# Hybrid encoder layer on one core: the expert row table built in fewer, larger steps and the last norm divided among three engines

## Chip, cores and metric

One core of a Trainium2 chip runs the whole program. The metric is the device time of one execution in microseconds, as the median of several runs.

## The reference, cut to what matters

The program is one layer of a streaming encoder over 1088 tokens (1024 of a prompt, 64 of a running stream) of width 1024, all in float32. Two token mixers (a state-space model and a sparse attention) end in a first layer norm. Behind it stands the part that the change touches:

```python
scores = sigmoid(x @ w_router)                       # 64 experts
idx    = top_k(scores + router_bias, 6)
gate   = scores[idx] / sum(scores[idx]) * 2.5
# each expert's rows are padded to whole blocks of 128 rows; one block uses one expert
out    = swiglu(x_pad[row_tok], w_exp_gu[e], w_exp_down[e]) * row_gate
routed = zeros.at[row_tok].add(out)
shared = swiglu(x, w_sh_gu, w_sh_down)
y      = layer_norm(ALPHA * x + routed + shared, ln2_g, ln2_b)
```

## The kernel before, in words

The five engines (PE, VectorE as DVE, ScalarE as ACT, GpSimd as POOL, and SyncE, whose queue SP issues most DMAs) each run an instruction list written by hand, and meet through semaphores. Tokens lie in NT = 9 tiles of 128 rows (the last has 64). The time from the first layer norm on has three stages.

**Shared tiles and row table.** For each tile i, PE multiplies the tile by the shared expert's first weights (`shared_up`, line 818), ACT takes the SiLU of one half, DVE multiplies by the other half (`gate_shared`, line 2122), PE turns the product (`turn_hidden`, line 800), ACT copies it out, PE multiplies by the second weights (`shared_down`, line 809), and DVE adds the result to x (`add_shared`, line 2139), after which SP stores the tile into `acc_d` in DRAM. PE's list is skewed: its pass i holds `shared_up(i+1)`, `turn_hidden(i-1)` and `shared_down(i-1)`.

Between these steps the table of rows is made. DVE first computes a slot for each (token, expert) pair (`slots`, `block_and_place`, lines 2178 to 2187). The slots become one-hot matrices: 54 products (6 picks of 9 tiles), for each of which DVE writes two parts (lines 2225 and 2226) and POOL one (line 1243) into a ring of 12 buffers, and PE adds them up in PSUM (line 856). From the thirteenth product on, DVE and POOL wait until PE has used the buffer that they overwrite. `planned_in(i)` says which products belong to DVE's pass i: 11 in each pass from pass 2 on, so that the last ten fall into pass 6, and into PE's pass 7. Then DVE copies the finished table out (line 2200), PE spreads it over partitions (line 866), DVE makes the row indices (lines 2207 and 2191), and POOL gathers the rows of the first blocks from DRAM by indirect DMA, four DMAs for one block (line 1259). DVE turns gathered rows with 32x32 transposes (`turn_rows`, line 2236).

**Expert loop.** Some 68 blocks, each with 16 matmuls of the first weights (`gate_and_up`, line 883), two transposes (line 889) and 8 matmuls of the second weights (line 897). SP loads 3 MB of weights for each block: the first weights of the block after next when PE is done with the buffer (`egu_full`), the second ones behind the previous block's last matmul. POOL gathers the rows of the coming block and adds the finished one to `acc_d` by an indirect DMA (line 1253).

**Last norm.** SP loads the nine tiles of `acc_d` back (`acc_loaded`). DVE makes mean and variance (`bn_stats` line 2065, `bn_aggr` line 2067, adding EPS line 2068), ACT the square root, DVE the reciprocal and shift (lines 2072 and 2073), ACT scales and shifts the tile (line 1610), DVE multiplies by `ln2_g` (line 2280), POOL adds `ln2_b` (line 1301), and SP stores the tile. All ACT instructions are put down to the helper's line 1307, and SP's loads to line 919.

The buffers `xg` and `xgT` (gathered rows and turned rows) lie over `x1T`, which the shared tiles read, so the first `turn_rows` stands behind the last `add_shared`. The one-hot ring is at offset 27712 of the arena:

```python
xg = [at(0, 4, 2 * P), at(1024, 4, 2 * P)]
xgT = [at(2048, DK, P), at(3072, DK, P)]
onehot = at(27712, 12, P + 2 * NBP)
```

## Time and profile before

| | |
|---|---|
| Median of 3 runs | 2145.34 us (2141.27 to 2145.65) |
| Profiled execution | 2142.77 us |
| Its span on the profile | 2140.8 us |
| PE busy | 1997.9 us (93%) |
| DVE, ACT, POOL busy | 972.6, 562.8, 617.2 us |
| DMA | 365.09 MB, mean 171 GB/s |
| Mean granted PE clock | 0.973 |

The span is one execution; its rows are in microseconds from the start of the span. A row of a timeline gives the start, the length, the engine, the line and the tiles, and in brackets how long the engine was idle before it and which instruction released it. Where several equal instructions are merged, "x8" is their number. PE's matmuls in float32 appear as two records for each product.

### The profile page before, as it was taken

How to read it: one execution, taken by the hardware profiler on the slowest of the kernel's cores; microseconds unless marked ns; L12 is line 12 of the kernel's file. 1: busy time of each engine (PE TensorE's matmuls, PEld its weight loads, DVE VectorE, ACT ScalarE, POOL GpSimd, SP SyncE). 2: the span in 40 equal slices, each digit the busy share in tenths (PEclk: the TensorE clock that was granted, in tenths of full speed). 3: DMA queues.
4: the chain of work that ended last, by engine and by line, in shares of the span. 5: the costliest groups of instructions: out<-in, count | busy, mean ns of one | idle time of the engine just before them, and what ended most of it. 6: DMA issues, size and time to landing. Idle time of an engine off the chain costs nothing.

```text
span 2140.8 us, 23579 instructions
## 1 busy us (share of the span) xinstructions
PE 1997.9 (93%) x7670; PEld 1105.0 (52%) x7670; DVE 972.6 (45%) x2561; ACT 562.8 (26%) x1136; POOL 617.2 (29%) x792
## 2 busy tenths in 40 slices
PE   8999999999999999998999798999999999999980
PEld 6786645666656665565454363444444444444430
DVE  4373465999755551240355543333323332333326
ACT  2224553661666630130223000111111111111112
POOL 0051000011210001101223253455555455545534
PEclk9999999999999999999999899999999999999995
DMA  5040212110100012024211403999999999999994
GB/s 184 3 46 5 62 40 99 40 50 0 32 19 2 1 45 55 19 94 126 111 67 53 155 30 113 362 374 372 374 380 376 374 372 375 378 374 373 372 336 176
DMA packets 130467, 365.09 MB, mean 171 GB/s; under 512 B 34641, under 2 KB 82514, under 8 KB 112594
## 3 DMA queue, kind: packets, MB, share of 16 engines
q1 hardware_dynamic: 105250, 289.80, 36.0%
q0 software_dynamic: 23328, 72.90, 13.1%
q10 hardware_dynamic: 1808, 1.33, 0.2%
q8 instruction: 48, 0.79, 0.2%
q14 instruction: 33, 0.27, 0.0%
HBM read 310.82 MB, written 53.04 MB: 170 GB/s over the span
## 4 chain that ended last, share of the span: by engine, by line
PE 54%; DMA 19%; DVE 9%; issue 7%; POOL 6%; ACT 3%; POOLq 0%; SPq 0%; DVEq 0%; ACTq 0%
DMA arena<-x_d,tid 17%; PE psum L606 11%; PE psum L747 8%; PE psum L765 6%; PE psum L621 4%; POOL arena L1259 3%; ACT arena L1307 3%; PE psum L428 3%; PE psum L818 2%; POOL acc_d L1253 2%; DVE arena L2236 2%; PE psum L682 2%; PE psum L701 2%; PE psum L463 2%; PE psum L474 2%
## 5 line engine op out<-in xcount | busy, mean ns | idle before, releaser
L1307 ACT ACTIVATE arena<-psum 128x512 f32<-128x512 f32 (+8 forms) x641 | 285.1, 485 | 1162.5 <-PE psum L883 436.0
L883 PE MATMUL psum<-arena 128*128 128x512 f32 x1088 | 486.1, 600 | 32.4 <-DVE arena L2236 25.9
L883 PEld LDWEIGHTS psum<-arena 128*128 128x128 f32 x1088 | 201.8, 190 | 273.9 <-issue 273.9
L1259 POOL DMA_INDIRECT arena<-x_d,tid x276 | 265.6, 962 | 83.2 <-issue 71.1
L897 PE MATMUL psum<-arena 128*128 128x512 f32 x544 | 244.7, 592 | 0.5 <-ACT arena L1307 0.5
L606 PE MATMUL psum<-arena 128*128 128x384 f32 (+1 forms) x768 | 239.7, 471 | 0.1
L2242 DVE TENSOR_TENSOR arena<-arena,psum 128x256 f32<-128x256 f32 x68 | 28.6, 421 | 462.6 <-ACT arena L1307 462.6
L606 PEld LDWEIGHTS psum<-arena 128*128 128x128 f32 x768 | 144.2, 190 | 95.4 <-issue 11.4
L747 PE MATMUL psum<-arena 128*128 128x384 f32 (+1 forms) x576 | 178.9, 474 | 5.9 <-DMA arena<-in_w_attn_proj 5.9
L2236 DVE STREAM_TRANSPOSE arena<-arena 128x256 f32<-128x256 f32 x272 | 150.2, 610 | 55.2 <-DMA arena<-x_d,tid 54.2
L897 PEld LDWEIGHTS psum<-arena 128*128 128x128 f32 x544 | 103.3, 190 | 130.3 <-issue 129.6
L1855 DVE TENSOR_SCALAR_CACHE_REDUCE arena<-arena 128x512 uint8<-128x512 f32 (+6 forms) x175 | 154.8, 929 | 2.0
L747 PEld LDWEIGHTS psum<-arena 128*128 128x128 f32 x576 | 110.7, 193 | 73.3 <-DMA arena<-in_w_attn_proj 6.4
L1265 POOL TENSOR_TENSOR carry<-ones 1x1 f32<-1x1 f32 x135 | 53.6, 397 | 314.1 <-DMA acc_d<-arena,sid 279.3
L1307 ACT ACTIVATE arena<-arena 128x896 uint8<-128x896 f32 (+1 forms) x99 | 110.5, 1117 | 77.6 <-DVE arena L1901 48.8
L1217 POOL TENSOR_TENSOR arena<-arena 128x384 f32<-128x384 f32 (+1 forms) x24 | 22.8, 951 | 362.3 <-DVE arena L2047 362.2
L765 PE MATMUL psum<-arena 128*128 128x512 f32 (+1 forms) x288 | 125.4, 594 | 1.6 <-POOL arena L1217 1.6
L1253 POOL DMA_INDIRECT acc_d<-arena,sid x68 | 111.1, 1633 | 11.5 <-POOL carry L1265 10.5
L1307 ACT ACTIVATE arena<-psum,gcol 128x512 f32<-128x512 f32 x68 | 46.7, 687 | 241.8 <-DVE gcol L2248 238.3
L1180 POOL TENSOR_TENSOR arena<-arena,rope 128x72 f32<-128x72 f32 (+3 forms) x72 | 29.5, 440 | 259.8 <-ACT iws L1307 185.6
L1199 POOL TENSOR_TENSOR arena<-arena 128x384 f32<-128x384 f32 (+1 forms) x24 | 23.8, 992 | 269.2 <-DVE arena L1965 269.2
L621 PE MATMUL psum<-arena 128*128 128x512 f32 (+3 forms) x288 | 94.3, 486 | 0.0
(306 smaller groups left out, 2265.3 us busy)
## 6 DMA issues: line engine op xcount, KB each, us to landing
arena<-in_w_exp_gu SPq DMA_DIRECT2D x69, 2048.0 KB, 10.4
arena<-in_w_exp_down SPq DMA_DIRECT2D x68, 1024.0 KB, 10.8
arena<-in_w_in SPq DMA_DIRECT2D x24, 512.0 KB, 4.5
arena<-in_x_prompt SPq DMA_DIRECT2D x10, 512.0 KB, 4.3
arena<-x_d,tid POOLq DMA_INDIRECT x276, 10.0
arena<-in_w_glu SPq DMA_DIRECT2D x16, 256.0 KB, 4.9
arena<-in_w_attn_proj SPq DMA_DIRECT2D x16, 256.0 KB, 4.5
arena<-in_w_out SPq DMA_DIRECT2D x1, 4096.0 KB, 13.0
```

The lines of the kernel that those rows point to most:

```text
L428: last = mm(psum[:, b, :], xT[:, k, t:SEQ:BL], w_u[:, k, :], start=k == 0, stop=k == DK - 1)
L606: last = mm(psum[:, b, 0:n], wgs[:, d % 2, w0 + k, :], src[:, k, t0:t0 + n], start=k == 0, stop=k == nk - 1)
L621: last = mm(psum[0:r, b, 0:n], xT[:, k, tok(i)], w_q[:, k, c0:c0 + n], start=k == 0, stop=k == DK - 1)
L747: last = mm(psum[:, b, 0:n], wap[:, w % 2, w0 + k, :], src[:, k, t0:t0 + n], start=k == 0, stop=k == nk - 1)
L765: last = mm(psum[0:r, banks.at[("wo", i)][0] + j, :], g1[:, k, tok(i)], w_o[:, k, j * 512:(j + 1) * 512], start=k == 0, stop=k == DK - 1)
L883: last = mm(psum[:, 2, :], xgT[u][:, k, :], ewg[u][:, k, :], start=k == 0, stop=k == DK - 1)
L897: last = mm(psum[:, 4 + 2 * u + j, :], ehT[u][:, k, :], ewd[u][:, k, j * 512:(j + 1) * 512], start=k == 0, stop=k == 1)
L1253: pool.indirect_dma_start(acc_d, bass.IndirectOffsetOnAxis(ap=sid[u][:, 0:1], axis=0), rows_, None, compute_op=ALU.add).then_inc(s(f"y_sto ...
L1259: pool.indirect_dma_start(xg[u][:, g, :], None, x1_d.rearrange("t (a f) -> (t a) f", a=4), bass.IndirectOffsetOnAxis(ap=tid[u][:, g:g + 1] ...
L1307: return act.activation(dst, src, fn, **kw)
L1855: ins = ts(hits[0:r, 0:n], score(i)[:, 0:n], thr[0:r, g:g + 1], None, op, ALU.add, accum_out=into[0:r, g:g + 1])
L2236: last = dve.transpose(xgT[u][:, :, 32 * g:32 * g + 32], xg[u][:, g, :].rearrange("p (j k) -> p k j", k=DK))
```

## The change

`planned_in` takes 18 products in each pass instead of 11, so that the 54 are issued in DVE's passes 2, 3 and 4 (PE's passes 3, 4 and 5). The copy of the table moves to DVE's pass 5, the spreading, the row indices and with them the first gathers to pass 6. `gate_shared(i)` moves one pass ahead on DVE. `xg` and `xgT` move to the offsets of the one-hot ring, which is no longer in use when the first gather starts; `turn_rows(0)` and the third index list stand in DVE's last shared pass, ahead of `add_shared(7)`, and `turn_rows(1)` ahead of the first `gate_up`.

In the last norm, the moments of tiles 1, 4 and 7 are taken by ACT, with a Copy and a Square that accumulate along the row and write their elementwise result to PSUM, where nobody reads it. DVE subtracts the mean and multiplies by `ln2_g` in one instruction (`scalar_tensor_tensor`), ahead of the scaling; ACT then multiplies by the reciprocal of the deviation; POOL still adds `ln2_b`. EPS goes in as the bias of the square root.

```diff
--- before.py
+++ after.py
@@ -215,8 +215,8 @@
 
         ewg = [at(15424, DK, 2 * DE), at(21568, DK, 2 * DE)]
         ewd = [at(15424 + 4096, 2, DM), at(21568 + 4096, 2, DM)]
-        xg = [at(0, 4, 2 * P), at(1024, 4, 2 * P)]
-        xgT = [at(2048, DK, P), at(3072, DK, P)]
+        xg = [at(27712, 4, 2 * P), at(28736, 4, 2 * P)]
+        xgT = [at(29760, DK, P), at(30784, DK, P)]
         yb = [at(4096, DM), at(5120, DM)]
         eh = at(6144, 4, DE)
         ehT = [at(7168, 2, P), at(7424, 2, P)]
@@ -224,6 +224,11 @@
 
         empty = at(49152, NBP)
         ln2 = at(10752, 2, DM)
+
+        fin = at(47104, NT, 6)
+        eps = at(47160, 1)
+        MOMENTS_BY_SCALAR = (1, 4, 7)
+        by_vector_no = lambda i: sum(j not in MOMENTS_BY_SCALAR for j in range(i + 1))
 
         ident = sb("ident", [P, P])
         tri = sb("tri", [P, P])
@@ -311,7 +316,7 @@
 
         block = ctx.enter_context(nc.Block())
 
-        planned_in = lambda i: range(max(0, 11 * (i - 2)), max(0, min(NT * MK, 11 * (i - 1))))
+        planned_in = lambda i: range(max(0, 18 * (i - 2)), max(0, min(NT * MK, 18 * (i - 1))))
         score_keys = lambda i: [(i, a0, n0) for a0, n0 in split(keys(i)[1], 512)]
         X_PARTS = ((0, 1), (1, 2), (2, 5), (5, NT - 1), (NT - 1, NT))
         x_part = lambda i: next(f"x_loaded{a0}" for a0, a1 in X_PARTS if a0 <= i < a1)
@@ -859,7 +864,7 @@
                             last.then_inc(s("onehot_used"), 1)
                         else:
                             filled(last, "tab")
-                    if i == NT - 1:
+                    if i == 6:
                         pe.wait_ge(s("tab_ready"), 2)
                         b = claim("tab4", "tab_ready", 3, pool=SIX)
                         for g in range(4):
@@ -1297,7 +1302,7 @@
             pool.wait_ge(s("ln2_loaded"), 32)
             for i in range(NT):
                 y = x1[0:rows(i), i, :]
-                pool.wait_ge(s("scaled"), i + 1)
+                pool.wait_ge(s("normed"), NT + i + 1)
                 tt(y, y, ln2[0:rows(i), 1, :], ALU.add).then_inc(s("out_ready"), 1)
 
 
@@ -1599,22 +1604,38 @@
             half_y(1, last_pair * 2 + 2)
 
 
+            moments = [0]
+
+            def moment(ins):
+                moments[0] += 1
+                ins.then_inc(s("moments"), 1)
+                act.wait_ge(s("moments"), moments[0])
+
             def final_std(i):
-                act.wait_ge(s("var_ready"), NT + i + 1)
-                f(lst[0:rows(i), (NT + i) % 2, 1:2], lst[0:rows(i), (NT + i) % 2, 0:1], ACT.Sqrt
-                  ).then_inc(s("std_ready"), 1)
-
-            def final_norm(i):
-                r, v = rows(i), (NT + i) % 2
+                r = rows(i)
+                m = lambda q: fin[0:r, i, q:q + 1]
+                if i in MOMENTS_BY_SCALAR:
+                    x, unread = x1[0:r, i, :], psum[0:r, 0:2, :].rearrange("p b n -> p (b n)")
+                    act.wait_ge(s(f"acc_loaded{i}"), 16)
+                    moment(f(unread, x, ACT.Copy, accum_out=m(4)))
+                    moment(f(m(5), m(4), ACT.Copy, scale=-1.0 / DM))
+                    moment(f(unread, x, ACT.Square, bias=m(5), accum_out=m(1)))
+                    f(m(2), m(1), ACT.Sqrt, scale=1.0 / DM, bias=eps[0:r, :]).then_inc(s("std_ready"), 1)
+                else:
+                    act.wait_ge(s("var_ready"), NT + by_vector_no(i))
+                    f(m(2), m(1), ACT.Sqrt, bias=eps[0:r, :]).then_inc(s("std_ready"), 1)
+
+            def final_scale(i):
+                r = rows(i)
+                act.wait_ge(s("scaled"), i + 1)
                 act.wait_ge(s("rstd_ready"), NT + i + 1)
-                f(x1[0:r, i, :], x1[0:r, i, :], ACT.Identity, bias=lst[0:r, v, 3:4],
-                  scale=lst[0:r, v, 2:3]).then_inc(s("normed"), 1)
-
-            for i in range(NT + 1):
+                f(x1[0:r, i, :], x1[0:r, i, :], ACT.Copy, scale=fin[0:r, i, 3:4]).then_inc(s("normed"), 1)
+
+            for i in range(NT + 2):
                 if i < NT:
                     final_std(i)
-                if i > 0:
-                    final_norm(i - 1)
+                if i >= 2:
+                    final_scale(i - 2)
 
 
         @block.vector
@@ -2191,17 +2212,26 @@
                 ts(tid[u][:], tab4[:, :, column].rearrange("p g n -> p (g n)"), 1.0, None,
                    ALU.mult).then_inc(s("tid_ready"), 1)
 
+            def turn_rows(u, loads):
+                dve.wait_ge(s(f"xg_loaded{u}"), loads)
+                for g in range(4):
+                    last = dve.transpose(xgT[u][:, :, 32 * g:32 * g + 32],
+                                         xg[u][:, g, :].rearrange("p (j k) -> p k j", k=DK))
+                last.then_inc(s("xgT_ready"), 1)
+
+            gate_shared(1)
             dve.wait_ge(s("x1_stored"), 16 * NT)
             for i in range(NT + 1):
-                if 0 < i < NT:
-                    gate_shared(i)
-                if i == NT - 2:
+                if 2 <= i + 1 < NT and i > 0:
+                    gate_shared(i + 1)
+                if i == 5:
                     await_bank(dve, "tab")
                     dve.tensor_copy(tab[:].rearrange("p a b -> p (a b)"), bank("tab")[:, 0:2 * NBP]
                                     ).then_inc(s("tab_ready"), 1)
                     dve.wait_ge(s("tab_ready"), 1)
                     step(ts(empty, tab[:, 0, :], 0.0, dump[:, 0:1], ALU.is_equal, ALU.mult))
                     stt(tab[:, 0, :], tab[:, 0, :], -1.0, empty, ALU.add, ALU.add).then_inc(s("tab_ready"), 1)
+                if i == 6:
                     dve.wait_ge(s("tab_ready"), 2)
                     await_bank(dve, "tab4")
                     ts(tab4[:].rearrange("p g n -> p (g n)"), bank("tab4")[:, 0:4 * NBP], 4.0, piece[:, 0:1], ALU.mult,
@@ -2209,6 +2239,9 @@
                     dve.wait_ge(s("tab_ready"), 3)
                     list_rows(0, slice(0, 1))
                     list_rows(1, slice(1, 2))
+                if i == NT - 1:
+                    turn_rows(0, 64)
+                    list_rows(0, slice(2, 3))
                 if i > 0:
                     add_shared(i - 1)
                 if i < 2:
@@ -2230,13 +2263,6 @@
 
             last_pair = dve.value_load(npair_i[0:1, 1:2], min_val=NE // 2 - 1, max_val=NBP // 2 - 1)
 
-            def turn_rows(u, loads):
-                dve.wait_ge(s(f"xg_loaded{u}"), loads)
-                for g in range(4):
-                    last = dve.transpose(xgT[u][:, :, 32 * g:32 * g + 32],
-                                         xg[u][:, g, :].rearrange("p (j k) -> p k j", k=DK))
-                last.then_inc(s("xgT_ready"), 1)
-
             def gate_up(u, blocks):
                 dve.wait_ge(s("esilu_ready"), blocks)
                 tt(eh[:, 2 + u, :], eh[:, u, :], psum[:, 2, DE:2 * DE], ALU.mult).then_inc(s("eh_ready"), 1)
@@ -2251,10 +2277,8 @@
                 ts(yb[u][:, 512:1024], psum[:, 5 + 2 * u, :], gcol[:, u:u + 1], None,
                    ALU.mult).then_inc(s("y_half"), 1)
 
-            turn_rows(0, 64)
-            list_rows(0, slice(2, 3))
+            turn_rows(1, 64)
             gate_up(0, 1)
-            turn_rows(1, 64)
             with dve.Fori(0, last_pair) as ip:
                 for u in range(2):
                     n = ip * 2 + u
@@ -2267,25 +2291,35 @@
             half_y(1, last_pair * 2 + 1, last_pair * 2 + 2, last_pair * 16 + 16)
 
 
-            def gather_up(i):
+            step(dve.memset(eps, EPS))
+
+            def final_moments(i):
                 r, x = rows(i), x1[0:rows(i), i, :]
                 dve.wait_ge(s(f"acc_loaded{i}"), 16)
-                variance(x, r, NT + i)
+                for q_ in range(2):
+                    last = dve.bn_stats(stats[0:r, i % 2, q_, :], x[:, q_ * 512:(q_ + 1) * 512])
+                step(last)
+                dve.bn_aggr(fin[0:r, i, 0:2], stats[0:r, i % 2, :, :].rearrange("p a b -> p (a b)")
+                            ).then_inc(s("var_ready"), 1)
 
             def scale_by_weight(i):
-                x = x1[0:rows(i), i, :]
+                r, x = rows(i), x1[0:rows(i), i, :]
                 if i == 0:
                     dve.wait_ge(s("ln2_loaded"), 32)
-                dve.wait_ge(s("normed"), NT + i + 1)
-                tt(x, x, ln2[0:rows(i), 0, :], ALU.mult).then_inc(s("scaled"), 1)
-
-            for i in range(NT + 2):
-                if i < NT:
-                    gather_up(i)
-                if 0 <= i - 1 < NT:
-                    scale_shift(rows(i - 1), NT + i - 1)
-                if 0 <= i - 2 < NT:
-                    scale_by_weight(i - 2)
+                if i in MOMENTS_BY_SCALAR:
+                    dve.wait_ge(s("std_ready"), NT + i + 1)
+                    stt(x, x, fin[0:r, i, 5:6], ln2[0:r, 0, :], ALU.add, ALU.mult).then_inc(s("scaled"), 1)
+                else:
+                    dve.wait_ge(s("var_ready"), NT + by_vector_no(i))
+                    stt(x, x, fin[0:r, i, 0:1], ln2[0:r, 0, :], ALU.subtract, ALU.mult).then_inc(s("scaled"), 1)
+                    dve.wait_ge(s("std_ready"), NT + i + 1)
+                dve.reciprocal(fin[0:r, i, 3:4], fin[0:r, i, 2:3]).then_inc(s("rstd_ready"), 1)
+
+            for i in range(NT + 1):
+                if i < NT and i not in MOMENTS_BY_SCALAR:
+                    final_moments(i)
+                if i > 0:
+                    scale_by_weight(i - 1)
 
 
 # ---- launch: one core; inputs and outputs as the reference has them ----
```

## Rows read from the trace of the kernel before

**Rows 1.** The page, the span in 40 slices: DMA share and GB/s.

```profile
DMA  5040212110100012024211403999999999999994
GB/s 184 3 46 5 62 40 99 40 50 0 32 19 2 1 45 55 19 94 126 111 67 53 155 30 113 362 374 372 374 380 376 374 372 375 378 374 373 372 336 176
```

**Rows 2.** Busy time by stretch, expert loop (us; busy of PE, PEld, DVE, ACT, POOL; PEclk; DMA share; GB/s).

```profile
1400.00:1500.00 100.00, 96.47 (x234) 43.55 (x233) 31.97 (x81) 12.12 (x27) 51.28 (x64) 1.00 1.03 374
```

**Rows 3.** Timeline of SP's DMA queue, start of the expert loop (start us, us, what).

```profile
1327.83 10.10 SPq L919 DMA_DIRECT2D arena<-in_w_exp_gu  x2
```

**Rows 4.** Timeline of PE, shared tiles to second block [idle before <-releaser].

```profile
1199.93 7.03 PE L818 MATMUL psum<-arena 128*128 128x512 f32 x16
1219.75 0.67 PE L800 MATMUL psum<-ident,arena 128*128 128x128 f32 x2 [12.79 <-DVE arena L2122]
1220.89 6.29 PE L809 MATMUL psum<-arena 128*128 128x512 f32 x8 [0.47 <-ACT arena L1307]
...
1234.12 4.51 PE L856 MATMUL psum<-arena 128*128 128x234 f32 x22
1238.47 3.60 PE L809 MATMUL psum<-arena 128*128 128x512 f32 x8
...
1305.66 3.67 PE L809 MATMUL psum<-arena 128*128 128x512 f32 x8 [2.64 <-issue]
...
1310.08 3.65 PE L809 MATMUL psum<-arena 128*64 128x512 f32 x8 [0.37 <-ACT arena L1307]
1318.30 8.80 PE L883 MATMUL psum<-arena 128*128 128x512 f32 x16 [4.57 <-issue]
1328.09 0.50 PE L889 MATMUL psum<-ident,arena 128*128 128x128 f32 x2 [0.99 <-DVE arena L2242]
1330.28 7.13 PE L883 MATMUL psum<-arena 128*128 128x512 f32 x16 [1.69 <-DVE arena L2236]
```

**Rows 5.** Timeline of DVE in the same stretch.

```profile
1219.18 0.42 DVE L2122 TENSOR_TENSOR arena<-arena,psum 128x256 f32<-128x256 f32 x1
...
1305.16 0.41 DVE L2122 TENSOR_TENSOR arena<-arena,psum 64x256 f32<-64x256 f32 x1
...
1313.83 1.21 DVE L2139 SCALAR_TENSOR_TENSOR arena<-arena,psum 64x1024 f32<-64x1024 f32 x1 [3.17 <-PE psum L809]
```

**Rows 6.** Timeline of POOL in the same stretch.

```profile
1219.26 9.05 POOL L1243 TENSOR_SCALAR arena<-iota,sblk,tokid 128x117 f32<-128x117 f32 x12 [36.01 <-DVE sin_ L2187]
...
1304.94 1.09 POOL L1259 DMA_INDIRECT arena<-x_d,tid  x1 [0.53 <-issue]
```

**Rows 7.** Busy time by stretch, where the first block begins (columns as rows 2).

```profile
1318.00:1320.00 2.00, 1.70 (x2) 0.83 (x3) 0.25 (x2) 0.00 (x0) 1.18 (x2) 0.58 0.00 0
```

**Rows 8.** Timelines of DVE, POOL and ACT, last norm.

```profile
2126.66 2.33 DVE L2073 SCALAR_TENSOR_TENSOR lst<-mv,lst 64x1 f32<-64x1 f32 x1
...
2130.30 3.32 DVE L2280 TENSOR_TENSOR arena<-arena 64x1024 f32<-64x1024 f32 x1 [0.17 <-ACT arena L1307]
...
2105.20 2.33 POOL L1301 TENSOR_TENSOR arena<-arena 128x1024 f32<-128x1024 f32 x1 [16.30 <-DVE arena L2280]
...
2126.64 2.34 POOL L1301 TENSOR_TENSOR arena<-arena 128x1024 f32<-128x1024 f32 x1 [1.23 <-DVE arena L2280]
2130.20 2.34 POOL L1301 TENSOR_TENSOR arena<-arena 128x1024 f32<-128x1024 f32 x1 [1.22 <-DVE arena L2280]
2133.70 2.33 POOL L1301 TENSOR_TENSOR arena<-arena 64x1024 f32<-64x1024 f32 x1 [1.16 <-DVE arena L2280]
...
2098.67 0.20 ACT L1307 ACTIVATE lst<-lst 128x1 f32<-128x1 f32 x1 [15.59 <-DVE lst L2068]
...
2100.58 1.24 ACT L1307 ACTIVATE arena<-arena,lst 128x1024 f32<-128x1024 f32 x1
```

**Rows 9.** Groups by line and form, ACT, whole span (count | busy us, mean ns of one | idle before).

```profile
L1307 ACT ACT_TABLE_LOAD x26 | 33.4, 1283 | 11.6 <-PE psum L747 10.4 <-PEq L2317 0.7
...
L1307 ACT ACTIVATION_READ_ACCUMULATOR arena<-arena,nbias 128x1 f32 x64 | 12.3, 192 | 0.0
```

## Prediction

> **What bounds the kernel now.** I read the page first, for its slices. From the expert loop on (slice 26, about 1338 us) the DMA share stands at nine tenths or more and the traffic at 362 to 380 GB/s, slice after slice, up to the last norm [rows 1]. The busy time by stretch says the same of 100 us of the loop: DMA share 1.03, 374 GB/s, and PE busy for 96.47 us with 234 first-weight and other matmul records, 26 to a block, so 9 blocks of 11.1 us each (66 or so from the second on) [rows 2]. The loop goes at the pace of its transfers, which this change doesn't lessen. What can be won lies ahead of it (the loop starts sooner) and behind it (the norm).
>
> Next the timeline of PE from the shared tiles on [rows 4]. After the third tile's first product (1199.93 + 7.03) PE stands for 12.79 us, until DVE's `gate_shared(1)`, which DVE does only when most of its slot work is through (1219.18 is the next gate, right behind the last slot) [rows 5]. From there PE is busy without a break until 1302. Then come three stalls: 2.64 us before `shared_down(7)`, which needs `gate_shared(8)`, done at 1305.57 behind DVE's wait for the table [rows 4, 5]; 4.57 us before the first block, since POOL gathers only from 1304.94 on [rows 4, 6]; and 0.99 and 1.69 us in the first block, the second because `turn_rows(1)` stands behind the first `gate_up` [rows 4].
>
> **Part 1, the start of the batches.** `gate_shared(1)` and `(2)` now stand ahead of slot work, so PE turns tile 1 at once (about 1207), does `shared_down(1)` in 3.6 us and `shared_up(4)` in 7.0, and has turned tile 2 at about 1218.5. DVE has one gate (0.42) more ahead of the last slot: slots end at 1219.18 + 0.42 = 1219.6. POOL starts its part at 1219.7 and takes 9.05 / 12 = 0.754 us for each [rows 6]; DVE, after one gate and one add (0.42 + 1.2), feeds its own parts from 1221.2 at a faster pace, so POOL sets it: 18 x 0.754 = 13.6, thus 1233.3, and PE's last product ends at 1233.7. The ring holds 12; the last six wait for PE's use, which keeps up. Before, PE was at this point at 1238.47, with only 11 products done [rows 4]: 4.7 us and seven products to the good.
>
> **Part 2, to the end of the shared tiles.** Before, PE went from 1238.47 to 1310.08 + 3.65 = 1313.73, or 75.3 us. Off go seven products at 4.51 / 11 = 0.4 (2.8 us) and the 2.64 wait: `gate_shared(8)` comes a pass earlier and no longer stands behind the table. On goes 0.6, because nothing covers ACT's copy in tile 6's turn any more (0.37 to 0.47 where it lies bare [rows 4]). That is 70.4 us. The later batches of 18: twelve are ready when PE comes (DVE has 7 us of `shared_up` for them), six follow POOL at 0.754 each from PE's first use, 4.5 us against the 4.9 that PE needs for twelve. No wait. PE ends at 1233.8 + 70.4 = 1304.2, against 1313.73: **9.5 us**.
>
> **Part 3, gathers and first blocks.** A pass of PE with a batch is 6.9 + 0.2 + 7.1 + 3.4 = 17.6 us, counted from start to start. From 1233.8, `shared_down(2)`, one whole pass and the next up to its batch put the complete table at 1269; after `shared_down(4)`, `shared_up(7)` and the transposes the spreading ends at 1280.5. From there to the first gather it was 1.9 us before (PE's idle time began at 1305.66 - 2.64 = 1303.0, the gather at 1304.94 [rows 4, 6]), so POOL gathers from about 1282.5. The eight DMAs of two blocks take about 10 us of issue (1.09 each and a gap), so the rows are there around 1293; `turn_rows(0)` ends near 1298.6, before `shared_down(7)` does (1299.8), and delays no add. The third block's rows are asked for at once, twenty us before they are used. The gathers write into the one-hot ring, dead by then. So the first block waits only for `add_shared(8)`: 1304.3 + 1.2, PE starts at about 1305.8 against 1318.30 (12.5 us). It took 8.80 us, not 7.13, with a granted clock of 0.58 between 1318 and 1320 after PE had been idle for 4.57 us [rows 4, 7], a mix of the 1.2 and 2.4 GHz levels; with an idle time of 1.6 I expect no such fall, and an end at 1312.9 instead of 1327.1 (14.2 us). The transposes come 1.0 later and last 0.5; the 1.69 wait is gone, as `turn_rows(1)` runs beside the first block. The second block starts at 1314.4, against 1330.28: **15.9 us**.
>
> SP's loop loads hang on these ends: two first-weight loads within 10.1 us from 1327.83 on, one behind each block [rows 3]. The first moves by 14.2, the second, with which the transfers fill up, by 15.9. The bytes in the loop stay the same, so its end moves with that start. I take 15.5 us.
>
> **Part 4, the last norm.** The rows show that DVE and POOL exclude each other in instructions that read two tensors from SBUF. A DVE instruction on one element per partition, started at 2126.66 beside POOL's add of 2126.64 to 2128.98, lasted 2.33 us; the multiplication at 2130.30, beside the add of 2130.20 to 2132.54, lasted 3.32, a little over 2.2 of waiting and 1.1 of work [rows 8]. POOL's adds follow each other at 3.56 us, 2.34 of add and 1.22 of idle in which DVE multiplies. The change keeps both: DVE's subtract-and-multiply also reads two tensors from SBUF, once a tile, and POOL still adds. What falls away is the small work between. ACT takes the first root at 2098.67 + 0.20; then tile 1's moments, 2 x (1.24 + 0.19) and a small negation 0.2, so 3.1 us; two roots 0.4; tile 0's scaling 1.24: POOL begins at 2103.7 instead of 2105.20 [rows 8, 9]. Nine adds follow at 1.2 + 2.34 = 3.55; the moments on ACT hold back a scaling for tiles 2 and 5, 0.4 and 0.8 us; the last add follows at 2.4, since its DVE part is done ahead of the add before. End: 2103.7 + 7 x 3.55 + 1.2 + 2.4 + 2.33 = 2134.4, less 0.3 where starts overlap, so 2134.0 against 2136.03: **2 us**. Loads and stores are as before.
>
> The Trainium skill, "SBUF — State Buffer", section "Who interferes with whom", has the rule: a DVE instruction with two SBUF inputs and a GpSimd instruction that reads SBUF take a shared port in turn, and the later one blocks fully. It speaks against this part of the change. By it the tail gives 2 us, without it 8; the rows above agree with it.
>
> **The sum.** 15.5 + 2.0 = 17.5 us. The profiled execution took 2142.77 us, 2.0 more than its span and 2.6 under the median shown; so 2125.3 for it and 2127.8 in the median's terms. I say 2127.5. Unseen costs: the clock while PE is fed at POOL's pace. After a 12.79 us idle time PE's 8 matmuls took 6.29 instead of 3.60 [rows 4]; if it falls again, the batch (PE then needs 0.8 for a product) and `shared_down(2)` cost up to 5 us, and nothing if not; the idle time is about 3 us, nearer the 4.57 after which it fell, so either is possible. ACT's Square and accumulation are bounded by 1.24 + 0.19 and by 1.28 more for each table load.
>
> **Rivals.**
> - *No exclusion for this DVE form.* Then POOL is fed by ACT and DVE alone and its adds come at 2.4 to 3 us: the tail gives 8 instead of 2, in all 2121.5. Against it: both forms in the rows above. Chance 0.08.
> - *Square needs another table than Sqrt.* A load takes 1.28 [rows 9], two for each of three tiles, 7.7 us on ACT; each holds up DVE's part of tiles 1, 4 and 7 and then POOL. The tail is then some 5 us longer than before instead of 2 shorter: about 2135. For it: no row has Square. Against: Copy, Identity and Sqrt, or Copy and Silu, alternate without loads. Chance 0.10. The Trainium skill ("ScalarE: Activation LUTs", "Table sets: the hidden batching unit") names relu, copy, identity and abs as in every set, and not Square; no row here decides it.
> - *The loop gives the lead back in part*: transfers start sooner but the first blocks, at PE's pace now, only meet the full queues sooner, and half is lost; 2135. Against: 374 GB/s is constant, so bytes decide, and the bytes move as a whole. Chance 0.08.
> - *Slower*: the loop settles in another order of scatter, gather and weight loads, and loses efficiency. From 17.5 / 66 = 0.27 us a block (2.4% of 11.1) it eats the gain, and at 0.4 the kernel takes 2154. Against: the rate is the same to 1 or 2% in every slice of the loop. Chance 0.04.
> - *The shared tiles are not earlier*: DVE, held in the ring for products 13 to 18, serves gates and adds too late, and PE waits about 1.5 us in each of three passes and the early gathers only save the stalls of the first block; 2136. Chance 0.06.
>
> **Chances and range.** The forecast, 2122 to 2133 with the clock and the spread of the runs, has 0.64; the rest as above. From 2119 to 2137 the range takes in all but the slower case and the outer edges. About 0.2% (4.3 us) can be told from no change. All cases but one (0.96) are faster by more than that; I move 0.05 of it to no change, for steps mis-sized together: faster 0.91, within 0.05, slower 0.04.
>
> **What would show it.** PE's 12.79, 2.64, 4.57 and 1.69 waits gone or under 2; the last `shared_down` ending near 1304; gathers from 1282; the second block at 1314; SP's loop loads from 1313.6; the last scatter some 15.5 earlier; POOL's adds still 3.5 us apart, and DVE's line for `scale_by_weight` at 1.2 us or, where blocked, up to 3.5. Wrong would be: adds at 2.4 us, table loads between the adds, a DMA rate in the loop under 370 GB/s, or PE waiting for POOL's one-hot parts in later passes.

## The result and the profile after

| | before | after |
|---|---|---|
| Median | 2144.66 us (4 runs, 2141.27 to 2145.65) | 2130.41 us (4 runs, 2129.55 to 2133.67) |
| Ratio | | 0.9939, 95% interval 0.9924 to 0.9954 |
| Profiled execution, its span | 2142.77, 2140.8 us | 2130.01, 2128.2 us |
| PE, DVE, ACT, POOL busy | 1997.9, 972.6, 562.8, 617.2 us | 2002.9, 970.8, 569.2, 621.0 us |
| Mean granted PE clock | 0.973 | 0.975 |

The change takes 14.3 us off. The page of the kernel after, its 40 slices (DMA share and GB/s; before: [rows 1]):

```profile
DMA  6041213110110011115311223999999999999995
GB/s 185 3 40 11 58 40 103 40 50 1 25 27 1 2 45 45 30 30 189 115 60 55 75 108 126 365 373 370 375 380 375 373 374 378 375 373 373 378 351 186
```

The loop runs as before: nine tenths and more, 351 to 380 GB/s. A stretch of 100 us in it (columns as in [rows 2]):

```profile
1400.00:1500.00 100.00, 95.86 (x234) 43.48 (x233) 31.91 (x81) 12.09 (x27) 51.33 (x62) 1.00 1.03 373
```

Now the timeline of PE from the fourth tile's `shared_up` on (`shared_up(3)`, tiles counted from 0), against [rows 4]:

```profile
1205.54 7.03 PE L823 MATMUL psum<-arena 128*128 128x512 f32 x16
1215.21 0.68 PE L805 MATMUL psum<-ident,arena 128*128 128x128 f32 x2 [2.64 <-DVE arena L2143]
1216.36 6.31 PE L814 MATMUL psum<-arena 128*128 128x512 f32 x8 [0.47 <-ACT arena L1312]
...
1229.60 3.39 PE L861 MATMUL psum<-arena 128*128 128x234 f32 x16
1233.27 0.63 PE L861 MATMUL psum<-arena 128*128 128x234 f32 x2 [0.28 <-DVE arena L2259]
...
1235.11 5.86 PE L861 MATMUL psum<-arena 128*128 128x234 f32 x16 [0.28 <-DVE arena L2259]
1240.80 3.60 PE L814 MATMUL psum<-arena 128*128 128x512 f32 x8
...
1251.33 7.28 PE L861 MATMUL psum<-arena 128*128 128x234 f32 x36
1258.44 3.60 PE L814 MATMUL psum<-arena 128*128 128x512 f32 x8
...
1303.82 3.70 PE L814 MATMUL psum<-arena 128*128 128x512 f32 x8 [0.47 <-ACT arena L1312]
...
1308.26 3.65 PE L814 MATMUL psum<-arena 128*64 128x512 f32 x8 [0.37 <-ACT arena L1312]
1313.28 7.13 PE L888 MATMUL psum<-arena 128*128 128x512 f32 x16 [1.38 <-DVE arena L2160]
...
1321.75 7.08 PE L888 MATMUL psum<-arena 128*128 128x512 f32 x16
```

Three of the four waits look as forecast: the 2.64 us before `shared_down(7)` are 0.47 (1303.82), the 4.57 before the first block (1313.28) are 1.38, the first block has run in 7.13 us instead of 8.80, and before the second one (1321.75) there is no wait. But of the 12.79 us a wait of 2.64 is left (1215.21), and `shared_down(1)` behind it still takes 6.31.

In the first pass with one-hot products (1229.60 to 1240.97) the records are torn by short waits. The rows name a DVE instruction as the releaser, but DVE has written its ninth part by 1230.9, and PE's ninth product starts at 1233.27. POOL's ninth, tenth and eleventh part end at 1233.12, 1234.04 and 1234.96, and PE goes on at 1233.27, 1234.19 and 1235.11, 0.15 us behind each: PE waits for POOL. DVE (`gate_shared(2)`) and POOL in this stretch, and the first weight loads of the loop, against [rows 5], [rows 6] and [rows 3]:

```profile
1214.64 0.42 DVE L2143 TENSOR_TENSOR arena<-arena,psum 128x256 f32<-128x256 f32 x1
```

```profile
1225.22 24.57 POOL L1248 TENSOR_SCALAR arena<-iota,sblk,tokid 128x117 f32<-128x117 f32 x30 [36.95 <-DVE sin_ L2208]
...
1290.03 1.09 POOL L1264 DMA_INDIRECT arena<-x_d,tid  x1 [0.53 <-issue]
```

```profile
1321.15 8.20 SPq L924 DMA_DIRECT2D arena<-in_w_exp_gu  x2
```

Last, the norm, against [rows 8]: DVE's subtract-and-multiply of two tiles, POOL's adds, ACT's moments.

```profile
2096.43 2.06 DVE L2314 SCALAR_TENSOR_TENSOR arena<-arena 128x1024 f32<-128x1024 f32 x1
...
2098.49 3.29 DVE L2314 SCALAR_TENSOR_TENSOR arena<-arena 128x1024 f32<-128x1024 f32 x1
...
2095.08 2.33 POOL L1306 TENSOR_TENSOR arena<-arena 128x1024 f32<-128x1024 f32 x1 [14.46 <-ACT arena L1312]
2097.96 2.73 POOL L1306 TENSOR_TENSOR arena<-arena 128x1024 f32<-128x1024 f32 x1 [0.55 <-ACT arena L1312]
2101.88 2.34 POOL L1306 TENSOR_TENSOR arena<-arena 128x1024 f32<-128x1024 f32 x1 [1.18 <-ACT arena L1312]
...
2114.81 8.56 POOL L1306 TENSOR_TENSOR arena<-arena 128x1024 f32<-128x1024 f32 x3 [0.30 <-ACT arena L1312]
...
2073.19 1.28 ACT L1312 ACT_TABLE_LOAD   x1
...
2090.73 1.01 ACT L1312 ACTIVATE psum<-arena 128x1024 f32<-128x1024 f32 x1
2091.68 0.19 ACT L1312 ACTIVATION_READ_ACCUMULATOR psum<-arena 128x1 f32 x1
...
2092.13 1.12 ACT L1312 ACTIVATE psum<-arena 128x1024 f32<-128x1024 f32 x1
```

**A table of stretches.** Single executions of one kernel differ by some us in places that nothing here changes: the instruction with which DVE copies the counts of the experts out of PSUM (I call it the count; line 2157 before, 2178 after), which closes a part of identical code, comes between 1194.2 and 1201.8 us in the eleven profiles of this study. In after's profile it comes at 1201.30, in before's at 1195.68. So I compare stretches, cut at the same four instructions: *shared* from the count to the second block's first matmul, *loop* from there to the start of the last block's down products, *scatter* to the norm's first `bn_stats`, *norm* to the end of the last add.

| kernel | shared | loop | scatter | norm | span |
|---|---|---|---|---|---|
| before | 134.60 | 748.73 | 17.91 | 39.11 | 2140.8 |
| after | 120.45 | 748.34 | 18.88 | 34.40 | 2128.2 |
| after_again | 120.48 | 750.00 | 17.68 | 34.42 | 2124.9 |
| tail_only | 134.72 | 751.45 | 18.67 | 34.41 | 2145.8 |
| gate_only | 123.57 | 751.81 | 18.66 | 39.09 | 2135.6 |
| gates_late | 129.47 | 749.90 | 18.05 | 34.41 | 2132.4 |
| g_in_psum | 120.45 | 749.54 | 18.22 | 29.24 | 2121.1 |
| gate2_first | 120.47 | 748.76 | 18.04 | 34.42 | 2120.7 |
| batches | 118.82 | 748.41 | 18.16 | 34.41 | 2122.6 |
| all_three | 118.82 | 749.92 | 17.96 | 24.64 | 2112.1 |
| iota_in_psum | 119.32 | 749.96 | 18.66 | 34.41 | 2126.6 |

A stretch whose code is the same repeats within 0.12 us in *shared* and 0.02 in *norm*; the loop varies by 3.5 whatever its start. By this table the change is worth 14.15 + 4.71 = 18.9 us, of which after's profile shows only 12.6 in the span: it lost 5.6 us ahead of the stretch and 0.6 in loop and scatter.

### The profile page after: what moved, and what is told of

It reads as the page before. It is cut to its first block, busy times and chain, and to the rows that moved or that the text cites. A ratio compares the mean times of both kernels' runs of the same rounds, so it can differ in the third digit from the quotient of the medians.

```text
span 2128.2 us, 23569 instructions
## 1 busy us (share of the span) xinstructions
PE 2002.9 (94%) x7670; PEld 1106.8 (52%) x7670; DVE 970.8 (46%) x2535; ACT 569.2 (27%) x1151; POOL 621.0 (29%) x792
## 4 chain that ended last, share of the span: by engine, by line
PE 56%; DMA 20%; issue 7%; DVE 7%; POOL 6%; ACT 3%; SPq 1%; POOLq 0%; DVEq 0%; ACTq 0%
DMA arena<-x_d,tid 16%; PE psum L611 11%; PE psum L752 8%; PE psum L770 6%; PE psum L626 4%; POOL arena L1264 3%; PE psum L433 3%; ACT arena L1312 2%; PE psum L823 2%; PE psum L687 2%; PE psum L706 2%; DVE arena L2218 2%; PE psum L468 2%; POOL acc_d L1258 2%; PE psum L888 2%
## 5 line engine op out<-in xcount | busy, mean ns | idle before, releaser
L888 PE MATMUL psum<-arena 128*128 128x512 f32 x1088 | 484.2, 598 | 28.1 <-DVE arena L2218 25.3
L2268 DVE TENSOR_TENSOR arena<-arena,psum 128x256 f32<-128x256 f32 x68 | 28.6, 421 | 457.6 <-ACT arena L1312 322.4
L611 PEld LDWEIGHTS psum<-arena 128*128 128x128 f32 x768 | 144.2, 190 | 95.7 <-issue 11.4
L1312 ACT ACTIVATE arena<-arena 128x896 uint8<-128x896 f32 (+4 forms) x120 | 123.3, 1034 | 103.8 <-DVE arena L1922 48.8
```

Of the source, the lines that this page charges most:

```text
L611: last = mm(psum[:, b, 0:n], wgs[:, d % 2, w0 + k, :], src[:, k, t0:t0 + n], start=k == 0, stop=k == nk - 1)
L888: last = mm(psum[:, 2, :], xgT[u][:, k, :], ewg[u][:, k, :], start=k == 0, stop=k == DK - 1)
L1312: return act.activation(dst, src, fn, **kw)
```

## The experiments

### The two halves of the change, and the early gates

**tail_only** is before with the new last norm alone. **gate_only** is before with the gates one pass ahead alone:

```diff
+            gate_shared(1)
             dve.wait_ge(s("x1_stored"), 16 * NT)
             for i in range(NT + 1):
-                if 0 < i < NT:
-                    gate_shared(i)
+                if 2 <= i + 1 < NT and i > 0:
+                    gate_shared(i + 1)
```

**gates_late** is after with these lines the other way round. What was expected of tail_only:

> The kernel before with the new last norm alone. Theory (the two parts add up): the shared tiles, gathers and loop as before, and from PE's last matmul to the end 58.1 us instead of 61.8, so 3.7 us less (3 to 5) than before; POOL's adds start some 6.1 us after DVE's first bn_stats instead of 8.3 and follow each other at 3.1 us on average instead of 3.56. Rival (the new norm is worth nothing, what the trace shows of it is an accident of one execution): within 1 us of before.

Measured: 2139.63 us in 12 runs, ratio 0.9978 (0.9965 to 0.9991), or 4.7 us less by the ratio and 5.1 by the medians. *Norm* is 34.41 instead of 39.11, *shared* is before's. POOL's first add begins 6.11 us after the first `bn_stats` in tail_only and in after, as expected, and the norm's gain neither needs the other half nor changes with it.

> The kernel before with gate_shared one tile ahead on DVE and nothing else: 11 products in a pass, table, buffers and norm as before. Theory (the early gates are the main gain, since shared_down(1) and shared_up(4) then run beside the slot work): PE's wait before turn_hidden(1) falls from 12.8 to 2.6 us, the shared tiles end about 9.5 us sooner and so does the kernel, 8 to 10.5 us. Rival (it is the larger passes and the early table that gain): 0 to 3 us.

Measured: 2134.98 us in 6 runs, ratio 0.9954 (0.9937 to 0.9970), or 9.9 less by the ratio; *shared* is shorter by 11.03. The timeline of PE in gate_only:

```profile
1225.93 5.68 PE L856 MATMUL psum<-arena 128*128 128x234 f32 x22
...
1300.19 3.65 PE L809 MATMUL psum<-arena 128*64 128x512 f32 x8 [0.37 <-ACT arena L1307]
1308.41 9.64 PE L883 MATMUL psum<-arena 128*128 128x512 f32 x16 [4.57 <-issue]
...
1321.23 10.07 PE L883 MATMUL psum<-arena 128*128 128x512 f32 x16 [1.69 <-DVE arena L2237]
```

The early gates alone bring the end of the shared tiles to 1303.84, or 106.2 us after the count, 11.9 earlier than before (118.1) where 9.5 had been expected. It is earlier than with the whole change, too (1311.91 - 1201.30 = 110.6). But then PE stands for 4.57, needs 9.64 us for the first block and stands again for 1.69: the granted clock between 1309 and 1311 is 0.50, the 1.2 GHz level. From the first block's start to the second's it is 12.82 us, in after 8.47. So the other edits of this half work against each other: with the passes of 18 and the early table the shared tiles end 4.4 us later, and what these make possible, `turn_rows` ahead of the last adds from buffers of their own, gives back 3.2 of wait and 4.35 in the first block. Net 3.1.

Of the 4.4, 2.9 lie in the first pass: with seven more products it ends 5.7 us later (39.5 us after the count against 33.8), where PE needs 2.8 for seven at the 0.40 of a later pass. The other 1.5 come behind it. And gate_only loses more to the clock than before does behind an equal wait of 4.57 us: its first two blocks take 9.64 and 10.07 us, before's 8.80 and 7.13. The second of them falls into its *loop*, the longest in the table. Why the same wait costs more there no run shows.

> The changed kernel with gate_shared in the passes where it stood before. Theory: PE waits 12.8 us before turn_hidden(1) again, then finds twelve products ready; the last shared_down ends at the time of before, less the 2.6 us wait, and the second block starts 8 us before that of the kernel before instead of 14; with 3.7 us of the norm it is 11 to 12 us under before, and 5 to 7 us over the changed kernel. Rival (the passes of 18 carry the gain): within 2 us of the changed kernel, 14 under before.

Measured: 2133.77 us in 7 runs, ratio 0.9949 (0.9931 to 0.9968), or 10.9 less. *Shared* is 129.47, so late gates cost 9.0 of the 14.15; 5.1 are left, and some 8 had been expected. PE in gates_late:

```profile
1219.81 0.67 PE L805 MATMUL psum<-ident,arena 128*128 128x128 f32 x2 [12.79 <-DVE arena L2143]
...
1293.86 7.08 PE L823 MATMUL psum<-arena 128*64 128x512 f32 x16 [1.71 <-DVE arena L2143]
...
1307.31 3.67 PE L814 MATMUL psum<-arena 128*128 128x512 f32 x8 [1.53 <-issue]
```

The 12.79 is back, and a wait that before does not have is new. In the late passes no one-hot products stand between PE's steps any more, so `shared_up(8)` reaches a late gate before DVE is done with it (1.71). And the 2.64 before `shared_down(7)` have shrunk to 1.53 (1307.31), not to nothing.

The two parts of the first half overlap: the early gates alone take 11.03 off *shared*, the rest alone 5.13, both together 14.15 and not 16.2. The norm's 4.7 comes on top in full.

### The same kernel once more

**after_again** is after without an edit.

> The changed kernel, unaltered, timed beside before on this chip. Theory (what the change touches is worth 18 to 19 us: 14.2 from the shared tiles to the second block and 4.7 in the norm; the 14.3 of the first comparison was lessened by chance ahead of the changed stretch, where its profiled execution was 5.6 us late): 16 to 19 us under before, and in the profile the same 120.4 us from DVE's first count instruction to the second block and 34.4 us of norm. Rival (the 14.3 is right, something earlier or in the loop is slower with the change): 13 to 15 us, and the stretch ahead late again by about 5 us.

Measured: 2127.02 us in 6 runs, before 2145.57 in 11, ratio 0.9916 (0.9898 to 0.9933), or 18.55 us less. *Shared* and *norm* are within 0.03 of after's; the count comes at 1197.58 instead of 1201.30. The first comparison gave 14.3, this one 18.55, the table 18.9: the intervals (9.9 to 16.3 and 14.4 to 21.9 us) just overlap, and the stretches that the change touches are the same. What makes identical code ahead of them vary by some us is not settled here.

### DVE's second operand in PSUM

**g_in_psum** is after with `ln2_g` copied once to PSUM, so that DVE's subtract-and-multiply reads only one tensor from SBUF:

```diff
+            act.wait_ge(s("ln2_loaded"), 32)
+            f(psum[:, 2:4, :].rearrange("p b n -> p (b n)"), ln2[:, 0, :]).then_inc(s("g_ready"), 1)
...
+                g_ = psum[0:r, 2:4, :].rearrange("p b n -> p (b n)")
                 if i == 0:
-                    dve.wait_ge(s("ln2_loaded"), 32)
+                    dve.wait_ge(s("g_ready"), 1)
...
-                    stt(x, x, fin[0:r, i, 0:1], ln2[0:r, 0, :], ALU.subtract, ALU.mult).then_inc(s("scaled"), 1)
+                    stt(x, x, fin[0:r, i, 0:1], g_, ALU.subtract, ALU.mult).then_inc(s("scaled"), 1)
```

> The changed kernel, with ln2_g copied by ACT into PSUM banks 2 and 3 after the loop, so that DVE's subtract-and-multiply reads one tensor from SBUF and one from PSUM. Theory (DVE and POOL exclude each other where DVE reads two tensors from SBUF): DVE's instruction lasts 1.2 to 1.3 us every time, never 2 or 3.3; POOL's adds 2.34, at 2.4 to 2.9 us; the norm ends 5 to 7 us sooner than in the changed kernel, 19 to 21 under before. Rival (ACT's moments and roots set the pace of the adds): DVE's instruction gets short, but the end moves by under 1.5 us.

Measured: 2119.37 us in 4 runs, ratio 0.9882 (0.9863 to 0.9901), or 25.3 us less. That is more than the 19 to 21 expected, which stood on the first comparison's 14.3; by the table it is 14.15 + 9.87 = 24.0. *Norm* falls from 34.40 to 29.24. DVE and POOL in it:

```profile
2095.74 1.26 DVE L2318 SCALAR_TENSOR_TENSOR arena<-arena,psum 128x1024 f32<-128x1024 f32 x1
...
2099.97 16.32 POOL L1306 TENSOR_TENSOR arena<-arena 128x1024 f32<-128x1024 f32 x7 [1.56 <-ACT arena L1312]
```

No instance of DVE's instruction lasts over 1.28 us now (after: up to 3.29), and POOL's last seven adds stand back to back, 16.32 / 7 = 2.33 us each. So it was the exclusion that held the adds at some 3.2 us a tile (eight steps from 2095.08 to 2121.04 in after). The Trainium skill, "SBUF — State Buffer", section "Who interferes with whom", says that a DVE instruction with at most one SBUF input does not contend with GpSimd, leaving its faster two-port modes aside; this pair of kernels agrees, with 1.28 against 3.29.

### The start of the table

The 12.79 us wait before the second `turn_hidden` was, by the code, not only a wait for its own gate: `turn_hidden(1)` takes a bank of PSUM that `gate_shared(2)` must have read. **gate2_first** moves that gate ahead too:

```diff
             gate_shared(1)
+            gate_shared(2)
             dve.wait_ge(s("x1_stored"), 16 * NT)
             for i in range(NT + 1):
-                if 2 <= i + 1 < NT and i > 0:
+                if 2 < i + 1 < NT:
                     gate_shared(i + 1)
```

> The changed kernel with gate_shared(2) ahead of the slot work too, so that turn_hidden(1) finds its PSUM bank free. Theory (the first pass of 18 is bound by POOL and DVE writing the one-hot parts side by side, PE only follows): the 2.6 us wait goes and PE's matmuls of shared_down(1) take 3.6 us, not 6.3, but PE then waits for the one-hot parts, and the stretch to the second block is 119.4 to 120.2 us instead of 120.45. Rival (PE's late start bounds the first pass): 115 to 117 us.

Measured: 2123.91 us in 6 runs, ratio 0.9903 (0.9885 to 0.9922), not to be told from after_again's. *Shared* is 120.47, as in after; 119.4 to 120.2 had been expected, and the rival's 115 to 117 is out. PE in gate2_first:

```profile
1206.18 3.70 PE L814 MATMUL psum<-arena 128*128 128x512 f32 x8 [0.47 <-ACT arena L1312]
...
1220.16 4.82 PE L861 MATMUL psum<-arena 128*128 128x234 f32 x14 [3.19 <-DVE arena L2260]
...
1228.02 5.88 PE L861 MATMUL psum<-arena 128*128 128x234 f32 x16 [0.28 <-DVE arena L2260]
```

The wait is gone (`shared_down(1)` at 1206.18 needs 3.70 us instead of 6.31), and another takes its place: 3.19 us before the first product, which cannot be there before DVE has all slots, and then POOL's pace again. POOL starts on its parts 23.9 us after the count in both kernels, and PE is through with the 18 products 39.7 us after it in both. The 2.64 us of after cost nothing.

**batches** deals the 54 products out as 11, 21 and 22, a smaller first pass:

```diff
-        planned_in = lambda i: range(max(0, 18 * (i - 2)), max(0, min(NT * MK, 18 * (i - 1))))
+        PASSES = (0, 11, 32, NT * MK)
+        planned_in = lambda i: range(PASSES[i - 2], PASSES[i - 1]) if 2 <= i <= 4 else range(0)
```

> The changed kernel with passes of 11, 21 and 22 products instead of 18, 18 and 18. Theory: the first pass costs PE 1.2 us more than its own matmuls instead of 4.1, the two larger ones less than 1 us each (the last ten in each follow POOL, at 0.84 us each from PE's first use on); the stretch to the second block falls from 120.45 to 117.5 to 119. Rival (the one-hot parts cost the same wherever they stand): 120 to 121 us.

Measured: 2123.95 us in 6 runs, ratio 0.9896 (0.9880 to 0.9913); *shared* is 118.82, 1.63 less than after's, inside the 117.5 to 119 expected.

```profile
1226.28 5.67 PE L862 MATMUL psum<-arena 128*128 128x234 f32 x22
...
1242.32 9.06 PE L862 MATMUL psum<-arena 128*128 128x234 f32 x42
...
1261.74 9.79 PE L862 MATMUL psum<-arena 128*128 128x234 f32 x44
```

Eleven products take 5.67 us where after's 18 need from 1229.60 to 1240.97, 11.4. The larger later passes cost little over PE's own pace: 9.06 / 21 and 9.79 / 22 are 0.43 and 0.45 us for a product, against 7.28 / 18 = 0.40 in after's second pass, so 0.6 and 0.9 us more in all. The first pass loses 1.2 us in this way instead of 4.1.

**iota_in_psum** is after with the source of DVE's two one-hot instructions copied to PSUM:

```diff
             gate_shared(1)
+            iota_ps = psum[:, 7, 0:P]
+            step(dve.tensor_copy(iota_ps, iota64[:]))
...
-                    ts(o[:, 0:P], iota64[0:r, :], sin_[0:r, m // MK, k:k + 1], None, ALU.is_equal)
-                    ts(o[:, P + NBP:], iota64[0:r, 0:NBP], sblk[0:r, m // MK, k:k + 1],
+                    ts(o[:, 0:P], iota_ps[0:r, :], sin_[0:r, m // MK, k:k + 1], None, ALU.is_equal)
+                    ts(o[:, P + NBP:], iota_ps[0:r, 0:NBP], sblk[0:r, m // MK, k:k + 1],
```

> The changed kernel, with the row of numbers that DVE compares against copied into PSUM bank 7, so that DVE's two one-hot instructions read no tensor from SBUF; POOL's part reads SBUF as before. Theory (POOL's part takes 0.82 to 0.83 us instead of 0.75 because DVE's SBUF-to-SBUF tensor_scalar keeps it waiting): POOL's products follow each other at 0.75 to 0.77 us also beside DVE's, and the stretch to the second block is 0.5 to 1.5 us shorter than 120.45, less 0.3 for the copy, if DVE's instructions keep their 0.28 and 0.34 us. Rival (POOL is slowed by PE's or the DMAs' traffic): still 0.82, and the stretch at 120.5 or longer.

Measured: 2125.81 us in 4 runs, ratio 0.9913 (0.9882 to 0.9944): as a time, no difference from after. In the stretch there is one: *shared* is 119.32, 1.13 less. The groups of POOL's and DVE's one-hot instructions by form (count | busy us, mean ns of one | idle before), first after, then iota_in_psum, then PE's first pass in iota_in_psum:

```profile
L1248 POOL TENSOR_SCALAR arena<-iota,sblk,tokid 128x117 f32<-128x117 f32 x48 | 39.0, 826 | 39.1 <-DVE sin_ L2208 37.0 <-PE psum L861 2.2
...
L2259 DVE TENSOR_SCALAR arena<-iota,sblk,gate 128x117 f32<-128x117 f32 x48 | 17.2, 358 | 0.0
...
L2258 DVE TENSOR_SCALAR arena<-iota,sin_ 128x128 f32<-128x128 f32 x48 | 13.6, 282 | 0.7 <-PE psum L861 0.7
```

```profile
L1248 POOL TENSOR_SCALAR arena<-iota,sblk,tokid 128x117 f32<-128x117 f32 x48 | 35.9, 760 | 40.0 <-DVE sin_ L2208 37.1 <-PE psum L861 2.8
...
L2261 DVE TENSOR_SCALAR arena<-psum,sblk,gate 128x117 f32<-128x117 f32 x48 | 18.6, 387 | 0.0
L2260 DVE TENSOR_SCALAR arena<-psum,sin_ 128x128 f32<-128x128 f32 x48 | 16.3, 339 | 0.0
```

```profile
1227.80 10.18 PE L861 MATMUL psum<-arena 128*128 128x234 f32 x36
```

POOL's part falls from 826 to 760 ns, DVE's rise from 282 and 358 to 339 and 387. In the first pass POOL takes 22.46 us for 30 instructions, 0.749 each, against 24.57, 0.819 each, in after; PE's 18 products are through in 10.18 us instead of 11.4, with no tear.

The 826 ns are a mean of two paces. The same group of POOL's in after, by the stretch in which its instructions lie: first between 1227.70 and 1234.90, while DVE writes its parts too, then between 1235.75 and 1246.10, while it writes none:

```profile
L1248 POOL TENSOR_SCALAR arena<-iota,sblk,tokid 128x117 f32<-128x117 f32 x8 | 7.3, 930 | 0.0
```

```profile
L1248 POOL TENSOR_SCALAR arena<-iota,sblk,tokid 128x117 f32<-128x117 f32 x14 | 10.5, 761 | 0.0
```

So beside DVE's instructions POOL's take 0.93 us, alone 0.76. In iota_in_psum they take 0.76 beside DVE's too. The rival, that PE's or the DMAs' traffic slows POOL, is out: in before they take 0.76 between 1221 and 1228, with the DMA share near 1 and DVE idle.

### All that helped, together

**all_three** is after with gate2_first, batches and g_in_psum; and `ln2_b` lies in PSUM too, so that DVE can take two of the nine adds while it has nothing else to do (ACT's unread results move to two other banks):

```diff
+        ADDS_BY_VECTOR = (6, 8)
...
+            f(psum[:, 0:2, :].rearrange("p b n -> p (b n)"), ln2[:, 1, :]).then_inc(s("tab_ready"), 1)
...
+            dve.wait_ge(s("tab_ready"), 5)
+            for i in ADDS_BY_VECTOR:
+                r, x = rows(i), x1[0:rows(i), i, :]
+                dve.wait_ge(s("normed"), NT + i + 1)
+                tt(x, x, psum[0:r, 0:2, :].rearrange("p b n -> p (b n)"), ALU.add).then_inc(s("onehot_ready"), 1)
```

> All of it: the changed kernel with gate_shared(2) first, passes of 11, 21 and 22, ln2_g and ln2_b in PSUM, and the adds of tiles 6 and 8 on DVE. Theory: the stretch to the second block takes 116.5 to 118.5 us; the norm ends 24 to 26 us after DVE's first bn_stats (29.2 with nine adds on POOL at 2.33; two fewer), so 30 to 32 us under before, about 2113. Rival (the norm is then bound by ACT or by the loads): 28 to 29 us of norm, 27 under before.

Measured: 2113.94 us in 5 runs (2112.56 to 2117.9), ratio 0.9857 (0.9839 to 0.9875). That is some 31 us under before and 13 under after_again on the same chip, the fastest version here. *Norm* is 24.64 (24 to 26 expected), *shared* 118.82 (116.5 to 118.5 expected, missed by 0.3: what gate2_first does adds nothing to batches). POOL and DVE at its end:

```profile
2095.58 11.74 POOL L1314 TENSOR_TENSOR arena<-arena 128x1024 f32<-128x1024 f32 x5 [1.56 <-ACT arena L1320]
...
2105.90 1.21 DVE L2341 TENSOR_TENSOR arena<-arena,psum 64x1024 f32<-64x1024 f32 x1 [0.62 <-ACT arena L1320]
```

POOL has five adds left at the end instead of seven, DVE does its two, operand in PSUM, in 1.2 us each where POOL takes 2.35.

## Why the prediction was right, point by point

The time, the range and the sign held. The forecast was a gain of 17.5 us; the stretches give 18.9, and the two comparisons 14.3 and 18.55. The 17.5 lie above the interval of the first comparison and inside that of the second. Its terms were less right than their sum, and that is partly luck: the shared part was put 1.4 us too high (15.5 against 14.15), the norm 2.7 too low, and the two errors offset each other in part.

**Part 1.** "`gate_shared(1)` and `(2)` now stand ahead of slot work, so PE turns tile 1 at once (about 1207)" failed. `gate_shared(2)` still stands behind most of the slots, done at 1215.06 by the timeline, and PE waits for it because of the bank. I had read the releaser's line in [rows 4, 5] and not which tile it served: before's row at 1219.18 is that gate already, not the "next" one (and the product at 1199.93 is the fourth tile's). `gate_shared(1)` was over at 1209.09, and PE stood on:

```profile
1208.67 0.42 DVE L2122 TENSOR_TENSOR arena<-arena,psum 128x256 f32<-128x256 f32 x1
...
1227.30 1.22 DVE L2139 SCALAR_TENSOR_TENSOR arena<-arena,psum 128x1024 f32<-128x1024 f32 x1 [7.69 <-PE psum L809]
```

A misreading without a price, as gate2_first shows. What was priced wrongly is POOL's pace: 18 x 0.754 after the gate of the last slot. The row of that price, 9.05 us from 1219.26 on, is from a stretch in which DVE stands idle for 7.69 us, as the second row above shows, and writes no one-hot part. With the early gates DVE is free to write its parts beside POOL's. So eight of POOL's 18 take 0.93 us and the 18 last 15.0 us, not 13.6. The first pass ended 39.5 us after the count (1240.80 - 1201.30) where I had 1233.8 - 1195.68 = 38.1: 1.4 us late. iota_in_psum shows DVE's SBUF reads as the cause, batches that the size of the first pass decides how much of it PE sees, and gates_late, where PE comes late and finds the ring full, that PE alone needs 7.28 for the 18 (from 1234.34 on).

The step "does `shared_down(1)` in 3.6 us" failed too: the loss of clock that I held possible came here. `shared_down(1)` took 6.31 as before, at a granted clock of 0.50 (1.2 GHz) between 1216 and 1218, behind the wait of 2.64; the one after the products took 3.60. It cost nothing either: in gate2_first it takes 3.70, and PE waits for the parts instead.

**Part 2.** 70.4 us was forecast, 1311.91 - 1240.80 = 71.1 measured. The period of a pass with a batch is 17.64 (1240.80 to 1258.44), as worked out, and PE waits for no one-hot part in the later passes. The 0.7 lie in two places: `shared_down(7)` (1303.82) waits 0.47 for ACT's copy where I had taken off the whole 2.64, and the pass with the third batch lasts 17.93.

**Part 3.** The wait before the first block is 1.38 (1.6 forecast), the block takes 7.13, with no fall of the clock, and the second block follows 8.47 us later (8.6 forecast). The first gather comes 88.7 us after the count (86.8 forecast); the eight of the first two blocks are issued by 1299.9, 12 us before the last `shared_down` ends, so they stay hidden. The second block gained 14.15, not 15.9; the difference is 1.4 of Part 1 and 0.7 of Part 2, less 0.2 here and 0.1 in the block. The reason given for the 4.57, "since POOL gathers only from 1304.94 on", was misread. Before's DVE ends its last add at 1315.04 and only then turns the first rows, as they lie over what the shared tiles read:

```profile
1316.02 2.18 DVE L2236 STREAM_TRANSPOSE arena<-arena 128x256 f32<-128x256 f32 x4 [0.97 <-DVE arena L2139]
```

PE starts at 1318.30, when they are turned. In gate_only the gathers begin 5.9 us before the last `shared_down` ends, in before 8.8, and the wait is 4.57 in both. What took it away is `turn_rows(0)` ahead of `add_shared(7)`, for which the early gathers are the condition. gate_only adds what the prediction did not say: with the gates early, the larger passes and the early table delay the shared tiles by 4.4 us, and only the stalls that they remove pay for them.

**The loop.** "The bytes in the loop stay the same, so its end moves with that start" held. The loop takes 748.3 to 751.8 us in all eleven profiles, whether it begins at 1315 or at 1337, at 373 GB/s in after's 100 us against 374. SP's first pair of weight loads begins 119.9 us after the count (1321.15), 12.3 earlier than before where 14.2 was forecast, and the first block ends 12.3 earlier, too. I had taken off 0.4 for the first weight load, and the table shows no such loss, though its spread of 3.5 could hide one. The rivals of a lead half given back and of a loop that settles otherwise are both out.

**Part 4.** The mechanism was right, its size was not: 4.7 us instead of 2. DVE and POOL exclude each other as the prediction read from [rows 8], and as the Trainium skill's rule has it ("SBUF — State Buffer", "Who interferes with whom"); DVE's instruction lasts 1.28 us ahead of the first add, and 2.06 and 3.29 beside an add. From POOL's first add to the end of its last it is 2123.37 - 2095.08 = 28.3 us. An estimate from two other runs comes near it: nine adds of 2.33 (g_in_psum, back to back) and seven multiplications of 1.08 (in before, the one at 2130.30 ends 1.08 after the add beside it) make 21.0 + 7.6 = 28.6. So the two engines work in turn; where POOL idles, as for 1.18 us before 2101.88, DVE multiplies. The term that failed is "Nine adds follow at 1.2 + 2.34 = 3.55": it has eight multiplications of 1.2 between the adds, and there are seven, of some 1.08, since those of tiles 0 and 1 are over before the first add. That makes 28.3 us instead of 30.3. The other 0.7 is the start: the first add comes 6.11 after `bn_stats`, 6.8 forecast, for the most part because the moments take ACT 2.7 us, not 3.1: its Copy to PSUM takes 1.01 and its Square 1.12 where I had 1.24 for both.

**The rivals.** No exclusion: out, by DVE's 3.29. Another table for Square: out, the trace has one table load, at 2073.19 ahead of the norm, and none between Copy, Square and Sqrt. Shared tiles not earlier because of the ring: out as a whole (7.4 us earlier by the count), though its mechanism, POOL's and DVE's pace, is what the first pass shows.

## What to carry to other kernels

Where two engines lock each other out, count their work as one queue, and look first for an operand that can lie in PSUM: one copy of 1 us took 5 us off this tail. Enlarging steps to finish earlier costs at the first step, which runs at the pace of whoever feeds it; make that one small and the later ones large. A price read from a stretch in which the neighbouring engine stands idle does not hold where both work. Before a wait is explained by the instruction that released it, look up which tile that instance served and which buffer the waiter claims.

## What the runs showed of the hardware that I had not expected

- POOL's one-hot instruction (128x117, float32) takes 0.76 us alone and 0.93 beside DVE's of the same kind when these read SBUF; beside DVE's that read PSUM it takes 0.76. DVE's own are faster from SBUF (0.282 and 0.358 us) than from PSUM (0.339 and 0.387). The Trainium skill, "SBUF — State Buffer", section "Who interferes with whom", says that `tensor_scalar`, too, can enter a mode in which it takes the pair of ports shared with GpSimd; the direction agrees, and the size here is 0.17 us on 0.76. Which mode DVE was in, the trace does not show.
- An ACT instruction with an accumulated sum costs 0.19 us more as a record of its own (`ACTIVATION_READ_ACCUMULATOR`), as in [rows 9]; its 1024-wide body takes 1.01 us for the Copy and 1.12 for the Square, which also reads one operand per partition.
- Stretches of identical instructions repeat within 0.02 to 0.12 us, while the loop, bound by DMA, and the 1200 us ahead of the change vary by 3.5 and 7.6 us from one execution to the next. A gain of 1 us as batches' or iota_in_psum's can be read in a stretch long before it can be timed.
